# A gate's weight conversion ahead of GpSimd's decay products, and a projection step between the scores of chunks 0 and 1

## What is computed

```python
b = jnp.cumsum(fb, axis=2)                       # fb: log f, with k = 1 - f
diff = b[:, :, :, None, :] - b[:, :, None, :, :]
decay = jnp.where(causal, jnp.exp(jnp.where(causal, diff, 0.0)), 0.0)
scores = jnp.einsum('bhtc,bhsc,bhtsc->bhts', qb, kb, decay)
o = jnp.einsum('bhts,bhsv->bhtv', scores, vb) + jnp.einsum('bhtc,bhcv->bhtv', qb * jnp.exp(b), s)
s_new = jnp.exp(b_last[:, :, 0, :])[..., None] * s + jnp.einsum('bhsc,bhsv->bhcv', kb * jnp.exp(b_last - b), vb)
...
merged = sigmoid(gate_sb) * o_sb + sigmoid(gate_hg) * (rms_norm(o_hg) * silu(hg_g))
```

## Time and profile before

| | us |
|---|---|
| median of 3 runs | 2565.75 (2564.24 to 2566.59) |
| the profiled execution | 2566.82 |
| its span, first to last instruction | 2562.7 |
| busy: TensorE, its weight load | 2360.8, 2121.8 |
| busy: VectorE, ScalarE, GpSimd | 1515.1, 1053.5, 1456.0 |

### The profile page before, as it was taken

How to read it: one execution, slowest core, us unless ns; L and a number is a source line. 1 busy time by engine, 2 the same in 40 slices (tenths; PEclk the granted TensorE clock), 3 DMA queues, 4 the chain that set the end, 5 groups by cost and what they waited for, 6 DMA issues and landing times. The chain is left out here.

```text
span 2562.7 us, 38184 instructions
## 1 busy us (share of the span) xinstructions
PE 2360.8 (92%) x14242; PEld 2121.8 (83%) x14242; DVE 1515.1 (59%) x2629; ACT 1053.5 (41%) x1735; POOL 1456.0 (57%) x1526
## 2 busy tenths in 40 slices
PE   4999999999999999999989699869999999999982
PEld 4889899898898998988969486559999999988982
DVE  7375775756757758567577576634444445444434
ACT  3442624525436245254362332213444444444334
POOL 6354564565646646555465445656666767776540
PEclk9999999999999999999999799989999999999996
DMA  5201111011111110111111432569999999999995
GB/s 177 67 26 42 43 39 55 26 41 49 33 36 47 37 53 26 43 47 35 34 38 76 157 132 67 147 145 289 321 320 333 340 341 346 346 346 351 358 345 186
DMA packets 210706, 380.65 MB, mean 149 GB/s; under 512 B 25794, under 2 KB 132670, under 8 KB 210010
## 3 DMA queue, kind: packets, MB, share of 16 engines
q1 hardware_dynamic: 180330, 302.31, 33.5%
q0 software_dynamic: 30192, 75.89, 12.7%
HBM read 310.78 MB, written 76.41 MB: 151 GB/s over the span
## 5 line engine op out<-in xcount | busy, mean ns | idle before, releaser
L125 PE MATMUL ps<-xTh,w_mix_low 128*128 128x368 f32 (+1 forms) x1728 | 595.6, 345 | 10.3 <-POOL w_mix_low L119 9.0
L126 PE MATMUL ps<-xTl,w_mix_high 128*128 128x368 f32 (+1 forms) x1728 | 568.9, 329 | 0.0
L127 PE MATMUL ps<-xTh,w_mix_high 128*128 128x368 f32 (+1 forms) x1728 | 566.7, 328 | 0.0
L2047 POOL DMA_INDIRECT xg_early<-h_d,tabq_early x310 | 317.7, 1025 | 107.3 <-issue 90.6
L125 PEld LDWEIGHTS ps<-xTh,w_mix_low 128*128 128x128 f32 x1728 | 325.7, 189 | 21.8 <-issue 18.5
L126 PEld LDWEIGHTS ps<-xTl,w_mix_high 128*128 128x128 f32 x1728 | 326.1, 189 | 9.1 <-issue 6.2
L127 PEld LDWEIGHTS ps<-xTh,w_mix_high 128*128 128x128 f32 x1728 | 325.6, 188 | 0.0
L2059 POOL DMA_INDIRECT ys_d<-yo,tab_early x114 | 213.2, 1870 | 186.4 <-DMA ys_d<-yo,tab_early 109.6
L1278 POOL TENSOR_TENSOR x_m<-x_m,kh_m 128x128 f32<-128x128 f32 (+1 forms) x272 | 127.0, 467 | 218.4 <-ACT x_m L831 218.4
L119 DVE TENSOR_TENSOR wdl<-wd_early,wdh 128x2048 fp32r<-128x2048 f32 x64 | 146.8, 2294 | 134.4 <-ACT wdh L114 84.0
L119 POOL TENSOR_TENSOR w_mix_low<-w_mix_raw,w_mix_high 128x1024 fp32r<-128x1024 f32 x72 | 174.7, 2427 | 88.8 <-ACT w_mix_high L114 88.5
(11 more groups left out here) (365 smaller groups left out, 4987.3 us busy)
## 6 DMA issues: line engine op xcount, KB each, us to landing
wd_early<-in_w_exp_down SPq DMA_DIRECT2D x64, 1024.0 KB
wg_early<-in_w_exp_gate SPq DMA_DIRECT2D x82, 512.0 KB
wu_early<-in_w_exp_up SPq DMA_DIRECT2D x82, 512.0 KB
w_mix_raw<-in_w_in SPq DMA_DIRECT2D x72, 512.0 KB, 3.8
wg<-in_w_exp_gate SPq DMA_DIRECT2D x42, 512.0 KB
wu<-in_w_exp_up SPq DMA_DIRECT2D x42, 512.0 KB
xg_early<-h_d,tabq_early POOLq DMA_INDIRECT x316
mT_d<-gs_m SPq DMA_DIRECT2D x8, 544.0 KB, 2.7
```

The lines of the kernel that those rows point to most:

```text
L125: pe.matmul(out, ll, rh, start=start, stop=False)
L126: pe.matmul(out, lh, rl, start=False, stop=False)
L127: return pe.matmul(out, lh, rh, start=False, stop=stop)
L2047: pool.indirect_dma_start(out=xg[:, b, g, :], out_offset=None, in_=h2_d[:, :].rearrange("t (q n) -> (t q) n", q=4), in_offset=bass.Indirec ...
```

## The change

It has two parts.

GpSimd, in `hgrn(h)`: the call of `split_due` that stood behind the multiplications of part 0 now stands ahead of everything else in the recurrent part. In heads 0 to 6 it converts the weights of gh; in head 7 those are converted within attention already, and it converts nothing. A second call, with the end of the first span, stands behind the multiplications of part 0. It converts the weights of gs, which before were converted behind part 1, by the call at the head of the loop over the chunks.

All of TensorE, ScalarE and VectorE: the last step of the first span, which stood ahead of products(0), stands behind them: gh 1 in heads 0 to 6, gh 0 in head 7. Its evacuation goes behind keys_out(0) and scores(0).

```diff
@@ TensorE, hgrn
-                    fill(S.hgrn[h][0])
+                    lo, hi = S.hgrn[h][0]
+                    fill((lo, hi - 1))
                     products(0)
+                    fill((hi - 1, hi))
                     for cn in range(NT):
@@ ScalarE, hgrn
                     exps(1)
-                    evacuate(lo + 2, hi)
+                    evacuate(lo + 2, hi - 1)
                     keys_out(0)
+                    evacuate(hi - 1, hi)
@@ GpSimd, hgrn
+                    split_due(S.hgrn[h][0][0])
                     pool.wait_ge(pa, PA * (h + 1))
                     pool.wait_ge(silu_done, 2 * h + 1)
                     times(0)
-                    split_due(S.hgrn[h][0][0])
+                    split_due(S.hgrn[h][0][1])
                     pool.wait_ge(qe_exp, h + 1)
                     pool.tensor_tensor(qe[:, :], qe[:, :], hq[:, h % 2, :], ALU.mult).then_inc(qe_done, 1)
                     times(1)
```

## The result

| | us |
|---|---|
| before, median of 4 | 2565.41 (2564.24 to 2566.59) |
| after, median of 4 | 2579.14 (2577.67 to 2581.70) |
| ratio after to before | 1.0051, interval 1.0039 to 1.0063 |
| the profiled execution of after | 2577.67, span 2572.9 |

13.7 us slower, where 5.6 us faster was forecast; the interval of the ratio leaves 1 out. Lines of after's kernel past the edits are 2 to 5 higher than before's (VectorE's cap L1009 is L1012, GpSimd's multiplication L1278 is L1282).

A forecast was written before the change was run, and what follows sets the result against it. TensorE was taken to bound the mixer (busy 164.14 of 170 us in a head). Gains -20.3, toll + 13.3 and head 7 + 1.45 gave -5.6 us, from 2565.75 to 2560.2 us; range 2553 to 2566.

The forecast's parts named there:

- The two gains: Heads 0 to 6: TensorE's stalls at the gate weights and between the chunks go, 1.45 us each, 20.3 us together.
- The toll: End of attention, heads 0 to 6: the conversion holds VectorE off the SBUF port, 1.9 us a head, 13.3 us together.
- the two orders: Who starts first at the SBUF port at attention's end: GpSimd, costing 2.25 us a head, or VectorE, 1.6; about even.
- GpSimd first: At attention's end the conversion starts ahead of VectorE's cap of unit 11; everything behind it moves by 2.25 us.
- The order not taken: VectorE's cap of unit 11 goes first, the conversion then holds its two scans; 1.6 us a head.
- Head 7: Products(2) wait for part 1 of x, less the gain between the chunks: + 1.45 us, bounds -1.5 and + 2.5.
- the sum: Whole kernel: -20.3 + 13.3 + 1.45 = -5.6 us, so 2560.2 us, bounds 2555.2 to 2564.8.
- rival (b): TensorE's clock falls at attention's end, dense steps lose 11.9 us: +6.3 in all, 2572 us; chance 0.06.
- the case in which a toll costs its own time and nothing more: Whole kernel: the forecast as worked out, 2555.2 to 2564.8 us; chance 0.74.

The follow-up runs named there:

- e4: Kernel after, with gh's first conversion behind VectorE's last scan of attention and gs's conversion back behind part 1: 2548.8 us, ratio 0.9915 to before.
- e5: Kernel after, with 12 unneeded matmuls in each of heads 0 to 6 ahead of TensorE's wait before unit 12's sums: 2569.5 us, ratio 1.0000 to before.
- e8: Kernel after, with GpSimd waiting for VectorE's cap of unit 11 ahead of the first conversion: 2570.6 us, ratio 1.0001 to before.
- e12: Kernel e8 once more, unchanged, one execution: 2560.1 us beside 2562.9 of before.

## Why the prediction was wrong, point by point

**The two gains: right.** Products(1) come 22.08 us behind the head's first hg matmul in heads with a full clock, 24.97 before: 2.9 us, as summed. e4 shows all of it: 166.4 for 169.4.

**The toll: the mechanism was right, the size at the upper end.** The middle of the two orders, 1.9, was taken, between 1.6 and 2.25. All seven places took the order GpSimd first, with 2.29 us of standing; e5 against e4 gives 2.2 us a head, 15.4 for 13.3. The order not taken was worth less than computed, 1.2 for 1.6.

**Head 7: right in kind.** The new wait at products(2) was foreseen, 28.1 us behind the first hg matmul for the 27.3 computed; its low half started 0.6 later than thought. From its first hg matmul to the end of the mixer head 7 takes 4.9 us more than before; + 1.45 was forecast. 2.2 of the 4.9 are there at products(2) (28.13 for 25.89), the other 2.7 come with the next chunk, at the low clock. That the clock would fall in the wait wasn't foreseen.

**The step that failed: the sum put the clock at nothing, and rival (b) got 0.06.** The runs show 13.1 us for it (after against e5). The rival was named with its place, but judged by "about as still as in 1336 to 1338", and the dense work on both sides was taken for protection. It also looked at too little of before's trace. A mean clock of 0.81 over 1336 to 1338 is 1.2 GHz from about 1337.2 on, so the last 0.8 us of that stretch are behind the fall. What stands 1.6 us ahead of it is a standstill of the very length that the toll was to bring:

```profile
1335.59 0.33 PE L609 MATMUL ps<-spl_m,trir 128*128 128x128 f32 x1 [2.29 <-DVE z_m L1009]
```

That doesn't make a fall certain (heads 0 and 5 of after had the same standstill and kept the clock), but it is far from 0.06. The stretch of 502 to 508 of before is thin work itself, in its busy time by stage:

```profile
502.00:508.00 6.00, 5.28 (x28) 3.56 (x27) 4.18 (x14) 2.50 (x8) 0.56 (x2) 1.00 0.00 0
```

28 matmuls in 6 us, most of them small, where a dense step starts one of 368 columns every 0.17 us; and the toll adds a full stop of 2.3 us to it. The clock fell in 5 of 7 heads in one profile and in 6 of 7 in the other.

The rival's price was near in total, 11.9 us, but by luck: 7 falls of 4 us at 1.7 us each were computed. after reaches head 7's first hg matmul 12.2 us later than e5 (1361.42 and 1349.19), with 5 falls of 6.8 to 10.2 us, 2.4 us for each; fewer and dearer. The other 0.9 of the 13.1 come in head 7 (last merge stored at 1443.05 and 1429.91).

**The sum with these sizes.** At the last merge: gains 7 x 2.9 = -20.3 (the masking of head 7 is in its own term), toll + 15.4, head 7 + 4.0 as in e5: - 0.9, which is e5 (1429.91 to 1430.85 in before). With the clock + 13.1 (of which 0.9 in head 7): + 12.2, which is after. e5's head 7 isn't free of the clock either: from products(2) to products(3) it takes 8.04 us for 6.41 in before, at 3.4 us of low clock. Without those 1.6 us the sum is - 2.5, where - 5.6 was forecast: 2.1 of the difference are the toll's, about 1 head 7's. The clock turned the sign of the sum. Between the profiled executions the difference is 10.9 us, by the medians 13.7. The 1.3 by which the first is under 12.2 lies behind the mixer, which the change doesn't touch. Where the 1.5 lies by which the second is over it, no trace shows.

**The chances.** 0.74 went to the case in which a toll costs its own time and nothing more. The standstill of TensorE was priced as time, and what it does to the clock only as a rival, though before's head 7 showed the two together.

## What to carry to other kernels

An idle engine isn't a free place: ask what each moment of its idle stretch shares with its neighbour. Here a GpSimd conversion of 2.34 us held a VectorE cap of 0.29 us, which reads two SBUF operands, for 2.46 us. Look for such pairs, and put the long instruction where VectorE has room (4 us later in the same hole turned + 13.7 us into - 17.0, and with gs's conversion back in its place into - 21.7), or cut it in two (- 9.8). And when a change makes TensorE stand inside thin work, price the clock as well as the standstill: here it fell at 11 of 14 such places, and cost 13.1 us, more than twice the gain that was forecast for the whole change.

## What the runs showed of the hardware that was not expected

- With starts 0.03 us apart (503.54 and 503.57) the engine that started first got the port, in all 7 places of after. The Trainium skill says so in "SBUF — State Buffer", section "SBUF: two separate sides"; the trace agrees, even at 0.03 us.
- The clock fell though TensorE never stood longer than 0.90 us at a time (e8), and on the same work it fell in one execution and not in another (head 4 of e8 and e12).
- Matmuls that compute nothing made the mixer 13.1 us shorter (e5 against after), 1.9 us for each 12 of them.
